# A two-block transformer kernel: layer 0's weight sums at other times, the output projection's first quarters split by depth, layer 1's first tiles copied raw, value weights summed on VectorE

## The reference, cut to what matters

```python
for l in range(2):                                    # first block, layers 0 and 1
    shift, scale, gate = split(silu(c) @ w_ada[l] + b_ada[l], 3)
    hx = rms_norm(x, norm_g[l]) * (1 + scale) + shift
    px = split_cols(hx @ w_in[l])                     # q, k, v, gate, conv a, conv b, ...
    u = c_a * sigmoid(c_b)                            # gated linear unit, then 31 conv taps
    y = concat([attn * silu(g_att), y_conv * silu(g_conv), y_four * silu(g_four)]) @ w_out[l]
    x = x + gate * y                                  # layer 0 does all this for ctx too
...
bv = (n @ w_in)[values of branch B]                   # second block: 1536 columns of values
# then three attentions, gates, and 16 experts with two per token, out = rms_norm(h, g)
```

## Time and profile before

| what | value |
|---|---|
| device time, median of 3 runs | 1044.68 us (1044.44 to 1046.56) |
| the profiled execution | 1046.3 us |
| its span | 1044.4 us |
| TensorE busy | 1013.3 us, 97% |
| VectorE, ScalarE, GpSimd busy | 440.3, 339.1, 97.7 us |
| DMA | 227.49 MB, mean 218 GB/s |

### The profile page before, as it was taken

The page is one execution under the profiler, slowest core; times in us unless marked ns, Lnnn a source line. Parts: engine busy times, 40 slices in busy tenths (PEclk is TensorE's granted clock), DMA queues, the critical chain, the costliest instruction groups (busy, mean ns, idle before and its releaser), DMA issues.

```text
span 1044.4 us, 14011 instructions
## 1 busy us (share of the span) xinstructions
PE 1013.3 (97%) x5196; PEld 707.3 (68%) x5196; DVE 440.3 (42%) x1236; ACT 339.1 (32%) x803; POOL 97.7 (9%) x148
## 2 busy tenths in 40 slices
PE   6999999998999999999999999999999999999996
PEld 2458654556887777888888877788888844444442
DVE  5579736456355665365845124932012420000004
ACT  5124234435053247245554124740111411111112
POOL 0160000033200000000006500000000020000000
PEclk9999999999999999999999999999999999999998
DMA  9963124762233422453444342049546699999996
GB/s 362 421 249 126 41 80 176 292 259 81 82 121 121 159 83 76 150 201 132 151 161 161 121 185 98 2 187 422 218 145 237 261 370 422 420 421 420 420 421 257
DMA packets 33936, 227.49 MB, mean 218 GB/s; under 512 B 4577, under 2 KB 4849, under 8 KB 8112
## 3 DMA queue, kind: packets, MB, share of 16 engines
q1 hardware_dynamic: 30784, 214.97, 52.8%
q10 hardware_dynamic: 1920, 9.80, 2.6%
q0 software_dynamic: 1168, 1.85, 0.5%
HBM read 222.15 MB, written 8.41 MB: 221 GB/s over the span
## 4 chain that ended last, share of the span: by engine, by line
PE 92%; DVE 3%; DMA 3%; ACT 1%; issue 1%; DVEq 0%; SPq 0%; POOL 0%; POOLq 0%; ACTq 0%
PE lin L579 21%; PE lin L1178 9%; PE sc L688 6%; PE aux L579 5%; PE sc L595 5%; PE aux L1178 5%; PE aux L1065 4%; PE sc L793 4%; PE lin L757 3%; PE aux L823 3%; PE sc L1143 3%; PE lin L809 3%; PE sc L579 3%; PE lin L595 3%; PE sc L972 2%; PE lin L839 2%
## 5 line engine op out<-in xcount | busy, mean ns | idle before, releaser
L579 PE MATMUL lin<-H,ring 128*128 128x256 f32 (+1 forms) x1008 | 222.8, 383 | 1.9 <-ACT PR L1544 1.9
L579 PEld LDWEIGHTS lin<-H,ring 128*128 128x128 f32 x1008 | 191.3, 190 | 32.0 <-issue 4.2
L688 PE MATMUL sc<-H,ring 128*128 128x512 f32 (+1 forms) x192 | 67.3, 496 | 0.0
L1395 ACT ACTIVATE SP<-lin 128x512 f32<-128x512 f32 (+2 forms) x88 | 42.2, 487 | 72.0 <-PE lin L809 71.9
L2001 DVE SCALAR_TENSOR_TENSOR UN<-UN,cols 128x512 f32<-128x512 f32 (+1 forms) x120 | 64.7, 612 | 0.0
L1406 ACT ACTIVATE SP<-SP,ST 128x513 f32<-128x513 f32 (+4 forms) x88 | 53.9, 612 | 6.5 <-DVE ST L1920 6.2
L688 PEld LDWEIGHTS sc<-H,ring 128*128 128x128 f32 x192 | 34.8, 189 | 30.3 <-issue 25.6
L1917 DVE CUSTOM_DVE_ANT_0 SP<-sc,CW,SK 128x512 f32<-128x512 f32 (+1 forms) x48 | 31.8, 662 | 55.4 <-PE sc L793 55.4
L2389 DVE TENSOR_TENSOR PR<-lin,PR 128x512 f32<-128x512 f32 x8 | 5.5, 692 | 94.6 <-PE lin L1178 94.6
L793 PE MATMUL sc<-PR 64*128 64x256 f32 (+3 forms) x240 | 42.2, 434 | 2.9 <-DVE ST L1917 2.1
L1065 PE MATMUL aux<-Y,ring 128*128 128x256 f32 x192 | 42.2, 380 | 0.5 <-DVE Y L1929 0.5
(11 more groups left out here) (423 smaller groups left out, 1590.3 us busy)
## 6 DMA issues: line engine op xcount, KB each, us to landing
ring<-w_stream SPq DMA_DIRECT2D x119, 1024.0 KB, 5.1
SP<-w_stream SPq DMA_DIRECT2D x13, 1024.0 KB, 21.8
UN<-w_stream SPq DMA_DIRECT2D x10, 1024.0 KB, 20.3
PR<-w_stream SPq DMA_DIRECT2D x8, 1024.0 KB, 22.4
CW<-w_stream SPq DMA_DIRECT2D x8, 1024.0 KB, 22.4
X<-w_stream SPq DMA_DIRECT2D x8, 1024.0 KB, 24.3
Y<-w_stream SPq DMA_DIRECT2D x8, 1024.0 KB, 19.0
PR<-ada_in SPq DMA_DIRECT2D x5, 1024.0 KB, 25.8
```

Source lines behind the costliest of these rows:

```text
L579: m = mm(dst, w[:, k, :], rhs(k), start=n == 0, stop=n == KT - 1)
L688: m = mm(bank[:, 0:ns * SEQ], filling["w"][:, k, :], H[:, 0:ns, k, :], start=k == 0, stop=k == KT - 1)
L1395: fn(PT[:, g % TURNED, a:b], take()[:, 0:b - a], ACT.Copy).then_inc(lin_taken, 1)
```

## The change

Four edits:

1. GpSimd's first group of layer 0's input weight sums also waits for the tokens of opening step 2, and its second and third for all four token sums `T_IN`.
2. In `paired_out`, each couple's two first products are done in two halves by depth: first the depths of branches 6 and 7 for both tiles, after two gated branches, then a wait for four, then the depths of 4 and 5. VectorE reads both first products before both second ones.
3. In layer 1 VectorE copies the tiles `CB` and `CB + 1` out of PSUM as they are, and ScalarE then applies the sigmoid in SBUF.
4. `mixed_values` moves from GpSimd to VectorE: four instructions of 1024 columns a group, the first group after the ropes, each next one between two additions of the group before it.

```diff
@@ out_at: order of the first two products
-            return 14 * (p // 2) + {1: 2 * x + 1, 5: 2 * x + 2, 2: 5 + x, ...}[product]
+            return 14 * (p // 2) + {1: 1 + x, 5: 3 + x, 2: 5 + x, ...}[product]
@@ TensorE, paired_out
-                        pe.wait_ge(gated, 4)
+                        pe.wait_ge(gated, 2)
                         pe.wait_ge(fill_taken, ADA_BLOCKS + len(FILLS[0]))
-                    quarter(alpha, w[p][:, 0, lo], YB[:, 4:8, 0, :]).then_inc(quarter_made, 1)
+                    for i in (2, 3):
+                        frees(mm(out_banks(p)[0], w[p][:, 0, lo][:, i * P:(i + 1) * P], YB[:, 4 + i, 0, :], start=i == 2, stop=False,
+                                 skip_group_check=True))
+                pe.wait_ge(gated, 4)
+                for p in couple:
+                    for i in (0, 1):
+                        m = mm(out_banks(p)[0], w[p][:, 0, lo][:, i * P:(i + 1) * P], YB[:, 4 + i, 0, :], start=False, stop=i == 1,
+                               skip_group_check=True)
...
+                    m.then_inc(quarter_made, 1)
+                for p in couple:
                     pe.wait_ge(tokens_mixed, 5)
                     pe.wait_ge(weights_mixed, 4 * (len(PAIRED) + p) + 1)
@@ ScalarE, layer 1's tiles
+                    for t in (CB, CB + 1):
+                        take()
+                        act.wait_ge(lin_taken, turn[L, t] + 1)
+                        fn(P1[:, t, 0, :], P1[:, t, 0, :], ACT.Sigmoid).then_inc(glu_gates, 1)
-                for t in TILES1:
+                for t in TILES1[2:] if layer == 1 else TILES1:
@@ GpSimd, layer 0's input weight sums
                 pool.wait_ge(fill_ready, 3 if n == 0 else 4)
+                if n == 0:
+                    pool.wait_ge(normed["l0"], 4 * 3)
+                    pool.wait_ge(shifted_x, 2 * 3)
+                else:
+                    pool.wait_ge(tokens_mixed, 4)
                 mixed(n, FIRST_PAIRED + n, *LO_HI, S_IN[n])
@@ VectorE, before layer 1's conv input
+                    for t in (CB, CB + 1):
+                        dve.wait_ge(lin_ready, turn[L, t] + 1)
+                        v.tensor_copy(P1[:, t, 0, :], lin[turn[L, t] % 2][:, 0:SEQ]).then_inc(lin_taken, 1)
+                    dve.wait_ge(glu_gates, 2)
@@ VectorE, value stage
+                        v.tensor_tensor(t1, lo[:, :, SEQ:512], lo[:, :, 0:SEQ], ALU.subtract).then_inc(weights_mixed, 1)
...
+                if t == BV:
+                    mixed_values(0)
...
                     v.tensor_tensor(BVT[:, 0, f0], BVT[:, 0, f0], beta, ALU.add).then_inc(quarter_added, 1)
+                    if g < 2:
+                        mixed_values(g + 1)
                     dve.wait_ge(quarter_read, V_READ + 5 * g + 4)
```

More of the change, by code:

```diff
@@ L384, in build @@
         quarter_made, quarter_read, quarter_added = (sem(n) for n in ("quarter_made", "quarter_read", "quarter_added"))
+        glu_gates = sem("glu_gates")
         idx_mask, merged, gains_ready = sem("idx_mask"), sem("merged"), sem("gains_ready")
@@ L431, in out_at @@
             x = p % 2
-            return 14 * (p // 2) + {1: 2 * x + 1, 5: 2 * x + 2, 2: 5 + x, 6: 7 + x, 7: 9 + x, 3: 11 + x, 4: 13 + x}[product]
+            return 14 * (p // 2) + {1: 1 + x, 5: 3 + x, 2: 5 + x, 6: 7 + x, 7: 9 + x, 3: 11 + x, 4: 13 + x}[product]
         def out_final(t):
@@ L637, in paired_out @@
                     w[p] = unit_of_pair()
-                    alpha, _, gamma = out_banks(p)
                     if p >= 2:
@@ L641, in paired_out @@
                     else:
-                        pe.wait_ge(gated, 4)
+                        pe.wait_ge(gated, 2)
                         pe.wait_ge(fill_taken, ADA_BLOCKS + len(FILLS[0]))
-                    quarter(alpha, w[p][:, 0, lo], YB[:, 4:8, 0, :]).then_inc(quarter_made, 1)
+                    for i in (2, 3):
[6 more added lines that the diff above has]
+                               skip_group_check=True)
+                        if i == 0:
+                            frees(m)
+                    m.then_inc(quarter_made, 1)
+                for p in couple:
                     pe.wait_ge(tokens_mixed, 5)
                     pe.wait_ge(weights_mixed, 4 * (len(PAIRED) + p) + 1)
-                    quarter(gamma, S_OUT[p][0], t1).then_inc(quarter_made, 1)
+                    quarter(out_banks(p)[2], S_OUT[p][0], t1).then_inc(quarter_made, 1)
                 pe.wait_ge(gated, KT)
@@ L992, in paired_values @@
                 pe.wait_ge(tokens_mixed, V_TOKENS + 4)
-                pe.wait_ge(weights_mixed, V_WEIGHTS + 8 * g + 6)
+                pe.wait_ge(weights_mixed, V_WEIGHTS + 4 * g + 3)
                 sixteenth(alpha, s2, t2, start=False).then_inc(quarter_made, 1)
@@ L1000, in paired_values @@
                 pe.wait_ge(quarter_read, V_READ + 5 * g + 4)
-                pe.wait_ge(weights_mixed, V_WEIGHTS + 8 * g + 8)
+                pe.wait_ge(weights_mixed, V_WEIGHTS + 4 * g + 4)
                 sixteenth(alpha, HB[:, 1, 4:8, :], t4, start=False).then_inc(quarter_made, 1)
@@ L1741, in _ @@
                         mixed(len(PAIRED) + n, FIRST_OUT + n, *LO_HI[::-1], S_OUT[n])
[L1743 to L1763, removed]
             nc.gpsimd.memset(MARK[:, 1:2], 0.0).then_inc(marked, 1)
@@ L2103, in _ @@
                             joined(p, 1, 0, 0, 2 * p)
+                        for p in (c, c + 1):
                             joined(p, 5, 2, 1, 2 * p + 1)
@@ L2153, in _, with mixed_values @@
                 if t == BK:
+                    def mixed_values(g):
+                        lo, hi = (ring[:, u % SLOTS, :, :].rearrange("p b (k n) -> p (b k) n", n=512) for u in (FIRST_V + 2 * g, FIRST_V + 2 * g + 1))
+                        for u in (FIRST_V + 2 * g, FIRST_V + 2 * g + 1):
+                            dve.wait_ge(unit_in[u % SLOTS], 16 * (u // SLOTS + 1))
+                        t1, t2, t4 = V_T[g]
+                        v.tensor_tensor(t1, lo[:, :, SEQ:512], lo[:, :, 0:SEQ], ALU.subtract).then_inc(weights_mixed, 1)
+                        dve.wait_ge(weights_mixed, V_WEIGHTS + 4 * g + 1)
+                        v.tensor_tensor(t2, hi[:, :, SEQ:512], t1, ALU.subtract).then_inc(weights_mixed, 1)
+                        v.tensor_tensor(lo[:, :, SEQ:512], hi[:, :, SEQ:512], lo[:, :, SEQ:512], ALU.subtract).then_inc(weights_mixed, 1)
+                        dve.wait_ge(weights_mixed, V_WEIGHTS + 4 * g + 3)
+                        v.tensor_tensor(t4, hi[:, :, 0:SEQ], t2, ALU.subtract).then_inc(weights_mixed, 1)
                     HB = H[:, 0].rearrange("p k (i two) -> p two k i", two=TT)
```

## The result

| | before | after |
|---|---|---|
| device time, median | 1046.45 us (5 runs, 1044.44 to 1048.5) | 1039.64 us (5 runs, 1039.36 to 1039.84) |
| ratio, 95% interval | | 0.9938 (0.9921 to 0.9954) |
| profiled execution, span | 1046.3, 1044.4 us | 1039.46, 1037.6 us |

What follows compares the result with a forecast made beforehand. TensorE, busy 97% of the span, was taken to bound the kernel. Gains of 1.8 + 1.7 + 1.9 + 0 = 5.4 us, off a median of 1044.68 us, gave 1039.3 us, range 1037.3 to 1041.9.

Steps and rivals of the forecast that it cites:

- Part 1: Opening: moving GpSimd's sums gains 3.21 us, a new TensorE wait at the second L915 costs 1.4; net 1.8 us.
- The turns: After the token sums, VectorE and GpSimd alternate one for one; six turns of 1.0 us cost VectorE 6.0 us.
- The Trainium skill's rule in its hardest reading: Shared SBUF ports: GpSimd's queued instructions always go first, VectorE getting through only when all eight are done.
- rival 1: No handing back after the opening: VectorE and GpSimd hardly meet, or L2026 is not late; 6.8 us gained, 1037.9; chance 0.12.
- rival 2: GpSimd always first after the opening: L915 stalls 1.5 us more, 3.9 us gained, 1040.8, or 1042.8; chance 0.15.
- Part 2: Output projection: half products fill TensorE's 2.1 us wait, leaving 0.3; gains 1.7 us, bounds 1.4 to 1.8.
- Part 3: Layer 1's third tile: TensorE's whole wait of 1.9 us is gained; bounds 1.5 to 1.9.
- Part 4: Value stage: no TensorE wait, 0 us; cover for VectorE's third-group sums is 12 us against 3.7 needed.
- Rival 4: Value stage: sums waiting for weights hold VectorE's queue, TensorE waits; slower, about 1047 us; chance 0.03.
- The end: Expert stage to stored rows: the DMA queue follows TensorE's progress, so the 5.4 us gained reach the end.
- Rival 3: Kernel end: the last weights' landing sets it and keeps its time, nothing gained, 1044.7 us; chance 0.06.
- The base: Starting time for the sum: the runs' median before, 1044.68 us, 1.6 lower than the profiled execution's 1046.3.

Runs made afterwards that it cites:

- only2: Kernel before, with only the output projection's first products done in halves: 1043.38 us, ratio 0.9971.
- only3: Kernel before, with only layer 1's first two tiles copied raw by VectorE: 1043.95 us, ratio 0.9979.
- only4: Kernel before, with only the value weights' sums moved to VectorE: 1046.35 us, ratio 0.9996.
- edits23: Kernel before, with the output projection's halves and layer 1's raw copies, without the other two edits: 1040.92 us, ratio 0.9953.
- wait_back: Changed kernel, the output projection's first halves waiting for four gated branches, not two: two runs at 1041.06 and 1041.42 us, four at 1042.55 to 1043.05.
- copies_back: Changed kernel, with layer 1's first tiles copied by ScalarE again: 1042.11, 1042.62, 1043.42, 1043.8 and 1044.28 us.
- values_behind: Changed kernel, with VectorE's sums for the third group of value weights issued behind that group's first addition: 1046.73 us.
- taps_later: Changed kernel, with four VectorE conv taps moved from ahead of the third pair's last two additions to behind them: 1038.36 us, ratio 0.9927.
- behind_scaling: Changed kernel, GpSimd's second group of weight sums waiting only for the last opening step's scalings, the third for nothing more: 1038.69 us, ratio 0.9919.
- group1_only: Changed kernel, with GpSimd's second and third group of weight sums where they were before, only the first group waiting: 1038.97 us.
- group3_late: Changed kernel, with GpSimd's third group of weight sums also waiting for VectorE's first addition of a pair: 1039.9 us.

## Why the prediction was right, point by point

**Part 1, 1.8 us.** Right in kind, with two sizes off. The gain of 3.21 us was read from one execution, in which `GS` took 1.28 us. In the traces of only2, only3, only4 and edits23, which have the old GpSimd sums too, the two steps were only 2.4 to 2.9 us longer than the clean ones, although their program is the same there: in the first of the two steps `GS` took 0.16, 0.18, 0.33 and 0.96 us, in the second 0.96 or 0.97 in all. The turns cost what was forecast: six for 9.4 - 3.4 = 6.0 us, as forecast, a wait of 0.97 us, 1.2 with its restart (forecast 1.4). Net it is 2.0 in the profiled pair, 2.6 - 1.2 = 1.4 from the middle of those traces, and 1.3 between edits23 and the changed kernel (1040.92 - 1039.64). The Trainium skill's rule in its hardest reading ("SBUF — State Buffer", "Who interferes with whom") did not hold: GpSimd had five instructions to go when VectorE began, and VectorE got its turn after each, 1.6 us a pair. The wait of 0.97 us at L926 speaks against rivals 1 and 2, which had none there and one of 2.9 us.

**Part 2, 1.7 us.** The wait was worth what was forecast, 1.75 between the traces; the clock was missed. wait_back's two runs without a fall lie 1.4 to 1.8 us above the changed kernel, its four others 2.9 to 3.4.

**Part 3, 1.9 us.** 2.2 in the traces of the changed kernel, copies_back and only3, over the stated bound of 1.9. A wait cost some 0.25 us more than the idle time that the view shows: 1.23 for 0.97 at L926, 2.2 for 1.94 here, 4.4 for 4.13 in values_behind. The clock was missed here too.

**Part 4, 0 us.** Right, and the cover too: with the sums taken behind it, the wait is 4.1 us of 4.2 forecast. Rival 4 falls: TensorE has no wait in that stage in only4 or the changed kernel.

**The end.** What was gained before 360 us was there at the last matmul. Rival 3 falls. But "it moves with it" was said too firmly: the landing of the stored rows ended the profiled execution of before 0.4 us late, and that of copies_back 0.8.

**The base.** The step that was wrong without harm, and the number was hit partly by luck: "the median of the runs was 1.6 us lower, 1044.68". Of those three runs two had no fall of the clock by their times; the profiled one had none either, and was high through its start, its opening and its end. Had the first three executions been usual ones, near 1046.45, the same sum would have given 1041.1, 1.4 us too high. Against the median of the 10 executions without a fall, 1044.83, the change is worth 5.2 us: 1.4 + 1.75 + 2.2 = 5.35 by its parts, 5.4 in the forecast's sum. Against the median of all, 1046.45, it is worth 6.8, and the other 1.6 us are one fall in a usual execution, which goes with the waits of 2.1 and 1.9 us. That after spreads over 0.5 us only fits this. The six kernels here without either wait (the changed one, edits23, taps_later, behind_scaling, group1_only, group3_late) each spread over 0.74 us at most, 30 executions in all, none with a mean clock under 0.997; the three at 0.997 are at most 0.7 us above their kernel's fastest, less than a fall. I had read the granted clock in the opening alone.

## What to carry to other kernels

When the runs of a kernel fall into clusters, compare their mean granted clock before building on one profile: a short wait of TensorE can cost its own length again behind it, in some executions and not in others, and closing it then gains both. When two engines slow each other, moving one's work costs the same number of turns elsewhere; put it where the slowed engine waits anyway, or do what another engine waits for ahead of what can come later. Read the length of a collision from several executions, not from one.

## What the hardware showed unexpectedly

The clock fell behind waits of 2.1, 1.9 and 4.1 us, for the first two in some executions and not in others of the same kernel; never behind the wait of 1.0 us at L926 in the six traces that have it. A fall costs 1.7 to 1.8 us, and comes behind a stretch without a break as well. And an instruction of 4 columns, `GS`, took from 0.16 to 1.28 us in openings with GpSimd's sums beside it, so a single profile can be off by up to one us for such a meeting.
